# Causal mask of the three-branch attention: added by VectorE head by head with the search for the smallest score, instead of by TensorE products

## The chip, the core and the metric

The kernel runs on one core of a Trainium2 chip. The metric is the time of one execution on the device, in microseconds. The kernel before takes 1296.79 us, the median of three runs (1296.17 to 1296.86).

## The reference, cut to what matters

The whole program is a chain of two blocks on 256 tokens of width 1024: four feed-forward layers, an mLSTM mixer, a three-branch attention ("nsa"), and two further attention mixers ("fox" and "dsa"). The change touches only the selected-block branch and the window branch of the three-branch attention. With 256 tokens the 4 blocks of 64 keys are all within the 16 that may be chosen, and the window of 512 covers everything, so both branches are causal attention over all keys, each with its own keys and values:

```python
m_s = (pos <= t[None, :, None, None, None]) & (val >= 0)[..., None]
s_s = jnp.einsum('bqhgd,bqhksd->bqhgks', qq, k_g).reshape(B, Q_BLOCK, N_KVH, G, top * SEL_BLOCK)
p_s = masked_softmax(s_s, m_s.reshape(B, Q_BLOCK, N_KVH, 1, top * SEL_BLOCK))
o_s = jnp.einsum('bqhgn,bqhnd->bqhgd', p_s.astype(dt), ...)
...
m_w = (kpos[None, :] <= t[:, None]) & (kpos[None, :] > t[:, None] - WINDOW) & (kpos[None, :] >= 0)
s_w = jnp.einsum('bqhgd,bkhd->bqhgk', qq, k_w)
p_w = masked_softmax(s_w, m_w[None, :, None, None, :])
o_w = jnp.einsum('bqhgk,bkhd->bqhgd', p_w.astype(dt), v_w)
return (gb[:, :, 0, :, :, None] * o_c + gb[:, :, 1, :, :, None] * o_s
        + gb[:, :, 2, :, :, None] * o_w)
```

There are 16 query heads in 4 groups that share keys, with 64 columns a head. `masked_softmax` subtracts the row's largest score, takes the exponential, sets masked places to 0 and divides by the row's sum. The kernel holds the scores with their sign turned, so it looks for the smallest and adds 1e30 where a key is masked.

## The kernel before, in words

The program is written by hand, engine by engine: each of TensorE, VectorE, ScalarE (ACT), GpSimd and SyncE has one list of instructions in fixed order, and semaphores tie the lists together. Nothing is scheduled by a planner. Most of the time goes to weight products: each weight piece is loaded, split by ScalarE into a high part (`whi`, line 1573) and by VectorE into a low part (`wlo`, line 2112), and multiplied by TensorE in three passes (lines 694, 695, 697).

The three-branch attention works in 12 units (`n_units`, line 493), here called unit 0 to unit 11. Units 0 to 3 belong to the first 128 tokens, one per key group; each holds 8 heads (4 of each branch) of 128 by 128 scores. Units 4 to 11 belong to the second 128 tokens, one per key group and branch; each holds 4 heads of 128 by 256 scores. A unit's scores fill two of PSUM's eight banks, half of the heads in each; even units have banks 0 and 1, odd units 2 and 3.

For each unit the engines do this:

- TensorE, `n_scores` (line 1305): two mask products (line 1320), which write the mask into the unit's two banks by multiplying a 128 by 128 identity with the mask, and then the heads' score products (line 1325), which add onto it. Identity and mask lie in the tile GH; ScalarE copies them there once (lines 1876 and 1877). From unit 2 on the products wait for the exponentials of the unit two before, which had the same banks.
- VectorE, `n_least_of` (line 2692): one reduction over the whole unit (line 2695), which gives the smallest score of each row and head.
- ScalarE, `n_exps` (line 1917): one exponential per head out of PSUM into SBUF (line 1924), with the row sums. All of them wait for the reduction.
- VectorE, `n_scale` (line 2697): reciprocal of the sums (2703), times the gates (2705 or 2708), and one product over the unit (2710).
- TensorE, `n_turn` (line 1329): eight transposes (line 1339) into banks 4 and 5. ScalarE copies the first out (line 1931), VectorE the second (`n_second_of_pt`, line 2715). Then `n_values` (line 1354) multiplies by the values.

VectorE's list in the loop (line 2730) is, for k from 0: scale unit k, least of unit k+2, copy of unit k's second transposed half; TensorE's is scores of unit k+2, transposes of unit k, values of unit k-1. Between these stand pieces of the third, compressed branch (lines 2665 to 2690 on VectorE, 1282 to 1303 on TensorE), and, once, the first half of the result leaves PSUM: after unit 4 TensorE's `cmp_values` (1301) ends the first 128 tokens' sums, ScalarE copies them out (1937), and VectorE takes their low part (2737). At the end stand, on TensorE, the transposes of units 10 and 11, the rest of the compressed branch, two values, and then the output projection.

The fox and dsa stages, later in the program, mask in another way: `mask_four` (line 2260) issues one `tensor_tensor_reduce` per head (line 2268), which adds the mask to a head's scores out of PSUM, writes the sums into SBUF and returns their smallest. In the trace this is a pair of instructions, CUSTOM_DVE_ANT_0 and DVE_READ_ACCUMULATOR2_ANT.

Of the kernel before, what the change touches and what calls it, by code (L numbers as in the profile page):

```python
# [19 lines left out]
ALU = mybir.AluOpType  # L20
ACT = mybir.ActivationFunctionType
AX = mybir.AxisListType.X

P = 128
# [15 lines left out]
BIG = 1e30  # L40
# [66 lines left out]
def program(nc, a, out):  # L107
# [20 lines left out]
    for name in order:  # L128
# [6 lines left out]
        else:  # L135
            w, chunks = stages[name]
# [5 lines left out]
    with ExitStack() as ctx:  # L142
        def sb(name, shape, dt=F32):
            return ctx.enter_context(nc.sbuf_tensor(name, shape, dt))

        def sem(name):
            return ctx.enter_context(nc.semaphore(name))
# [13 lines left out]
        GH = sb("GH", [P, 2, T], F32R)  # L161
# [23 lines left out]
        nmin = sb("nmin", [P, 96])  # L185
# [11 lines left out]
        ident = con[:, C_ID:C_ID + P]  # L197
        caus = con[:, C_CAUS:C_CAUS + 256]
# [4 lines left out]
        def carve(start, *sizes):  # L203
            views, at = [], start
            for n in sizes:
                views.append(arena[:, at:at + n])
                at += n
            assert at <= AW, (at, AW)
            return views
# [17 lines left out]
        KTS, VTS, KB, VB, v_k, v_kd, v_cd, v_ct, v_sc, v_scT = carve(  # L227
            0, 2 * KVH * T, 2 * NT * T, KVH * 64, 2 * KVH * P, 1024, 2048, 2048, 2048, 256, 256)
        KTS = KTS.rearrange("p (b h t) -> p b h t", b=2, h=KVH)
# [140 lines left out]
        q_ps = sem("q_ps")  # L370
        n_ps = sem("n_ps")
        n_in = sem("n_in")
        n_const = sem("n_const")
        n_score = sem("n_score")
        n_least = sem("n_least")
        n_exp = sem("n_exp")
# [114 lines left out]

        q_bank = (0, 1, 4, 5)
        n_units = [(0, g, None) for g in range(KVH)] + [(1, g, b) for g in range(KVH) for b in range(2)]
        n_ident, n_later = GH[:, 0, 0:P], GH[:, 0, P:2 * P]

        def n_bank(t, c):

# [2 lines left out]
        def n_rows(k):  # L500

            return (8, P) if k < KVH else (4, T)

        def n_cols(k):

            at = 8 * k if k < KVH else 4 * k + 4 * KVH
            return slice(at, at + n_rows(k)[0])

        def n_slot(k, b, j):

            return 4 * (j % 2) + 2 * b + j // 2 if k < KVH else 2 * (j % 2) + j // 2

        def n_score_banks(k):

            n, w = n_rows(k)
            return PS[:, 2 * (k % 2):2 * (k % 2) + 2, :].rearrange("p b n -> p (b n)").rearrange("p (j s) -> p j s", j=n)

        def n_weights(k):

            n, w = n_rows(k)  # L520
            return wide[:, 1024 * (k % 2):1024 * (k % 2) + 1024].rearrange("p (j s) -> p j s", j=n)
# [160 lines left out]
        def _(pe):  # L682
            mm, tr = nc.tensor.matmul, nc.tensor.transpose
# [392 lines left out]
            o = side("m_rows")  # L1076
# [8 lines left out]
            for name, sums in (("m_a", (grow[2], grow[0])), ("m_floor", (grow[1],))):  # L1085
                o = side(name)
# [218 lines left out]
            def n_scores(k):  # L1305

                t, g, one = n_units[k]
                if k == 0:
                    pe.wait_ge(n_const, 1)
                    pe.wait_ge(n_in, 4)  # L1310
                elif k == 1:
                    pe.wait_ge(n_in, 6)
                else:
                    pe.wait_ge(n_exp, k - 1)
                if k == KVH:
                    pe.wait_ge(qT_act, 2)
                    pe.wait_ge(qT_dve, 2)
                o, (n, w) = n_score_banks(k), n_rows(k)
                for m in range(2):
                    mm(o[:, n // 2 * m:n // 2 * m + n // 2, P * t:P * t + P], n_ident,  # L1320
                       n_later.unsqueeze(1).to_broadcast([P, n // 2, P]), start=True, stop=False, skip_group_check=True)
                for b in range(2) if one is None else (one,):
                    for j in range(4):
                        half = slice(64 * (j % 2), 64 * (j % 2) + 64)
                        last = mm(o[:, n_slot(k, b, j), :], n_qT[half, 2 * g + j // 2, t * P:t * P + P],
                                  KTS[half, b, g, 0:w], start=False, stop=True, skip_group_check=True)
                last.then_inc(n_score, 1)

            def n_turn(k):
# [66 lines left out]
            k = len(n_units) - 2  # L1396
# [16 lines left out]
            o = side("f_rows")  # L1413
# [35 lines left out]
            for t in range(NT):  # L1449
                for c in range(3):  # L1450
                    n, end = stages["dsa"][1][c][2], chunk_end("dsa", c)
                    if t == 0 and c == 0:
# [4 lines left out]
                        o = PS[:, dsa_bank(0, 0), 0:n]  # L1457
# [21 lines left out]
            for w in range(2):  # L1479
                o = side(f"qi{w}")  # L1480
                for i in range(2):
                    for t in range(NT):
                        m = 2 * w + i
# [4 lines left out]
            o = side("kr")  # L1488
# [3 lines left out]
            o = side("ki_ckv")  # L1492
# [32 lines left out]
            for j in range(4):  # L1525
                o = side(f"dk{j}")
                for i in range(2):
                    last = mm(o[:, i * T:i * T + T], d_wukr[:, 2 * j + i, :], d_ckvT, start=True, stop=True,
                              skip_group_check=True)
# [29 lines left out]
        def _(act):  # L1559
            A = nc.scalar.activation  # L1560
# [157 lines left out]
            o = even_bank("mlstm", 0)  # L1718
# [12 lines left out]
            o = side("m_rows")  # L1731
# [10 lines left out]
            o = even_bank("mlstm", 3)  # L1742
            A(m_qT[:, 0:2, :], two(o), ACT.Copy).then_inc(chunk_act, 1)
            o = side("m_floor")
# [16 lines left out]
            o = even_bank("mlstm", 4)  # L1761
# [40 lines left out]
            o = even_bank("kv", 0)  # L1802
# [70 lines left out]


            turn("nsa")
            A(n_ident, ident, ACT.Copy)
            A(n_later, caus[:, P:2 * P], ACT.Copy).then_inc(n_const, 1)
            root_of("nsa")
            first = first_piece["nsa"]

# [36 lines left out]
            def n_exps(k):  # L1917

                if k >= 2:
                    act.wait_ge(n_turned, k - 1)  # L1920
                act.wait_ge(n_least, k + 1)
                o, c = n_score_banks(k), n_cols(k).start
                for j in range(n_rows(k)[0]):
                    last = A(n_weights(k)[:, j, :], o[:, j, :], ACT.Exp, scale=-1.0, bias=nmin[:, c + j:c + j + 1],
                             accum_out=zsum[:, c + j:c + j + 1])
                last.then_inc(n_exp, 1)
# [51 lines left out]
            o = even_bank("fox", 0)  # L1978
            A(f_f[:, 0, :], o[:, 336:344], ACT.Copy)
            A(f_v[:, 0, 688:1024], o[:, 0:336], ACT.Copy).then_inc(chunk_act, 1)  # L1980
            o = even_bank("fox", 1)
# [9 lines left out]
            o = side("f_rows")  # L1991
            A(grow[1], o[0:HEADS, 0:T], ACT.Identity, bias=bif[:, 2:3]).then_inc(side_act, 1)
            log_forget(1)
            o = even_bank("fox", 2)
            A(f_v[:, 0, 344:688], o[:, 0:344], ACT.Copy).then_inc(chunk_act, 1)
            silu_sigmoid("fox", 3, 0)
            for c in (4, 5):
                o = even_bank("fox", c)
                A(f_qT[:, 4 * (c - 4):4 * (c - 4) + 2, :], two(o), ACT.Copy, scale=-float(P) ** -0.5)\
                    .then_inc(chunk_act, 1)  # L2000
            for c in (6, 7):
                o = even_bank("fox", c)
# [40 lines left out]
            o = side("qi0")  # L2043
            A(d_qiT[:, 0:2, :], two(o), ACT.Copy).then_inc(side_act, 1)
            o = even_bank("dsa", 3)
            A(xs[:, 0, 512:1024], o, ACT.Copy).then_inc(chunk_act, 1)
            o = side("ki_ckv")
# [21 lines left out]
            for j in (0, 2):  # L2069
                o = side(f"dk{j}")  # L2070
# [4 lines left out]
            for j in range(4):  # L2075
                if j == 2:
                    exps_four("dsa", 0)
                o = side(f"dv{j}")
# [19 lines left out]
        def _(dve):  # L2098
            V = nc.vector
# [257 lines left out]
            o = odd_bank("mlstm", 0)  # L2357
# [60 lines left out]
            o = side("m_a")  # L2418
# [3 lines left out]
            o = odd_bank("mlstm", 3)  # L2422
# [12 lines left out]
            o = odd_bank("mlstm", 4)  # L2435
# [83 lines left out]
            o = odd_bank("kv", 0)  # L2519
# [171 lines left out]

            def n_least_of(k):

                dve.wait_ge(n_score, k + 1)
                V.tensor_reduce(nmin[:, n_cols(k)], n_score_banks(k), AX, ALU.min).then_inc(n_least, 1)

            def n_scale(k):

# [67 lines left out]
            o = odd_bank("fox", 0)  # L2766
            V.tensor_copy(f_f[:, 1, :], o[:, 336:344])
            V.tensor_copy(f_v[:, 1, 688:1024], o[:, 0:336]).then_inc(chunk_dve, 1)
            o = odd_bank("fox", 1)
# [26 lines left out]
            o = odd_bank("fox", 2)  # L2796
# [13 lines left out]
            for c in (4, 5):  # L2810
                o = odd_bank("fox", c)
# [5 lines left out]
            for c in (6, 7):  # L2817
                o = odd_bank("fox", c)
# [89 lines left out]
            o = side("qi1")  # L2908
# [16 lines left out]
            o = side("kr")  # L2925
# [54 lines left out]
            for j in (1, 3):  # L2980
                o = side(f"dk{j}")
# [61 lines left out]
```

## Time and profile before

| what | us |
|---|---|
| median of the runs | 1296.79 |
| the profiled execution | 1295.36 |
| its span, first to last instruction | 1293.6 |
| TensorE busy in the span | 1267.7 |
| VectorE busy | 872.2 |
| ScalarE busy | 615.9 |

The profiled execution is one execution with the hardware profiler on; its time is the device's, and its span is what the trace covers. The units of the change stand from about 766 to 824 us of the span. TensorE counts as busy while a product is in its pipeline, so a busy TensorE is not one at its peak; its clock has two levels, 1.2 and 2.4 GHz, which the profile shows as a granted share of 0.5 and 1. On VectorE an instruction's duration overlaps the next one's start by some 0.07 us, so the time that an instruction takes from its engine is read from start to start.

### The profile page before, as it was taken

How to read it: one execution, taken by the hardware profiler on the slowest of the kernel's cores; microseconds unless marked ns; L12 is line 12 of the kernel's file. 1: busy time of each engine (PE TensorE's matmuls, PEld its weight loads, DVE VectorE, ACT ScalarE, POOL GpSimd, SP SyncE). 2: the span in 40 equal slices, each digit the busy share in tenths (PEclk: the TensorE clock that was granted, in tenths of full speed). 3: DMA queues.
4: the chain of work that ended last, by engine and by line, in shares of the span. 5: the costliest groups of instructions: out<-in, count | busy, mean ns of one | idle time of the engine just before them, and what ended most of it. 6: DMA issues, size and time to landing. Idle time of an engine off the chain costs nothing.

```text
span 1293.6 us, 16507 instructions
## 1 busy us (share of the span) xinstructions
PE 1267.7 (98%) x6723; PEld 1075.0 (83%) x6723; DVE 872.2 (67%) x1314; ACT 615.9 (48%) x842; POOL 19.2 (1%) x35
## 2 busy tenths in 40 slices
PE   8999999999999999999999998999999999999997
PEld 6888888988888888888888876788888899988876
DVE  7655557887655557685757669765555567576896
ACT  6434436535434446454544456664344353544471
POOL 2000000100000000000000000000000000000000
PEclk9999999999999999999999989999999999999999
DMA  9665545444655555566574340065555686446401
GB/s 330 222 195 194 182 149 185 162 140 153 214 186 195 187 184 164 181 196 199 174 245 165 135 163 1 15 226 180 179 185 192 133 225 173 146 140 221 162 1 66
DMA packets 158812, 218.17 MB, mean 169 GB/s; under 512 B 8257, under 2 KB 110993, under 8 KB 158737
## 3 DMA queue, kind: packets, MB, share of 16 engines
q1 hardware_dynamic: 157168, 213.33, 51.3%
q0 software_dynamic: 1376, 3.71, 1.0%
q8 instruction: 53, 0.87, 0.3%
q14 instruction: 23, 0.18, 0.0%
q10 hardware_dynamic: 192, 0.08, 0.0%
HBM read 216.04 MB, written 1.05 MB: 168 GB/s over the span
## 4 chain that ended last, share of the span: by engine, by line
PE 88%; DVE 7%; ACT 1%; issue 1%; DMA 1%; SPq 1%; DVEq 0%
PE PS L694 25%; PE PS L697 24%; PE PS L695 24%; PE PS L729 2%; PE PS L736 2%; PE PS L730 2%; PE PS L844 2%; PE PS L714 1%; DVE wlo L2112 1%; PE PS L1055 1%; PE PS L1339 1%; DMA raw<-in_ffn_w_out_dram 1%; DVE arena L2710 1%; SPq L602 1%; DVE d_work L2959 1%
## 5 line engine op out<-in xcount | busy, mean ns | idle before, releaser
L2112 DVE TENSOR_TENSOR wlo<-raw,whi 128x2048 fp32r<-128x2048 f32 (+4 forms) x205 | 455.1, 2230 | 125.5 <-ACT whi L1573 124.9
L1573 ACT ACTIVATE whi<-raw 128x2048 fp32r<-128x2048 f32 (+4 forms) x205 | 379.6, 1864 | 69.2 <-DMA raw<-in_fox_w_in_dram 32.3
L694 PE MATMUL PS<-whi,XL 128*128 128x512 f32 (+4 forms) x976 | 378.2, 388 | 2.2 <-DVE wlo L2112 1.3
L695 PE MATMUL PS<-wlo,XH 128*128 128x512 f32 (+4 forms) x976 | 372.6, 383 | 0.0
L697 PE MATMUL PS<-whi,XH 128*128 128x512 f32 (+4 forms) x976 | 259.5, 383 | 0.0
L694 PEld LDWEIGHTS PS<-whi,XL 128*128 128x128 f32 x976 | 183.4, 188 | 36.4 <-DVE wlo L2112 2.1
L695 PEld LDWEIGHTS PS<-wlo,XH 128*128 128x128 f32 x976 | 183.6, 188 | 32.4
L697 PEld LDWEIGHTS PS<-whi,XH 128*128 128x128 f32 x976 | 181.7, 189 | 34.6
L1629 ACT ACTIVATE scr<-PS,rn 128x256 f32<-128x256 f32 x88 | 41.7, 474 | 224.4 <-PE PS L697 223.9
L694 PE MATMUL PS<-whi,GL 128*128 128x512 f32 x320 | 125.4, 392 | 0.0
L695 PE MATMUL PS<-wlo,GH 128*128 128x512 f32 x320 | 124.6, 389 | 0.0
L2212 DVE SCALAR_TENSOR_TENSOR scr<-PS,rn,scr 128x256 f32<-128x256 f32 x88 | 42.4, 482 | 92.6 <-ACT scr L1629 92.4
L697 PE MATMUL PS<-whi,GH 128*128 128x512 f32 x320 | 98.7, 390 | 0.0
L1634 ACT ACTIVATE GH<-PS 128x512 fp32r<-128x512 f32 x40 | 23.9, 599 | 156.4 <-PE PS L844 156.4
L694 PE MATMUL PS<-XH,wlo 128*128 128x256 f32 x320 | 81.5, 287 | 1.2 <-ACT xs L2079 1.2
L695 PE MATMUL PS<-XL,whi 128*128 128x256 f32 x320 | 80.2, 283 | 0.0
L2221 DVE TENSOR_TENSOR GL<-PS,GH 128x512 fp32r<-128x512 f32 x40 | 27.7, 691 | 73.7 <-ACT GH L1634 73.6
L697 PEld LDWEIGHTS PS<-whi,GH 128*128 128x128 f32 x320 | 60.1, 188 | 12.6
L695 PEld LDWEIGHTS PS<-wlo,GH 128*128 128x128 f32 x320 | 60.1, 188 | 12.1
L694 PEld LDWEIGHTS PS<-whi,GL 128*128 128x128 f32 x320 | 60.1, 188 | 12.2
L694 PEld LDWEIGHTS PS<-XH,wlo 128*128 128x128 f32 x320 | 61.3, 192 | 2.9 <-ACT xs L2079 2.0
L695 PEld LDWEIGHTS PS<-XL,whi 128*128 128x128 f32 x320 | 61.3, 192 | 0.1
(402 smaller groups left out, 1360.3 us busy)
## 6 DMA issues: line engine op xcount, KB each, us to landing
raw<-in_ffn_w_in_dram SPq DMA_DIRECT2D x174, 512.0 KB, 4.9
raw<-in_ffn_w_out_dram SPq DMA_DIRECT2D x88, 512.0 KB, 4.9
raw<-in_fox_w_in_dram SPq DMA_DIRECT2D x24, 512.0 KB, 8.1
raw<-in_a_w_in_dram SPq DMA_DIRECT2D x16, 512.0 KB, 4.5
raw<-in_dsa_w_in_dram SPq DMA_DIRECT2D x16, 512.0 KB, 4.9
raw<-in_kv_w_dram SPq DMA_DIRECT2D x12, 512.0 KB, 4.2
raw<-in_fox_w_in_dram SPq DMA_DIRECT2D x12, 344.0 KB, 5.1
raw<-in_a_w_out_dram SPq DMA_DIRECT2D x8, 512.0 KB, 4.6
```

Of the source, the lines that this page charges most:

```text
L694: mm(o, xl, wh, start=start and i == 0, stop=False, skip_group_check=True)
L695: mm(o, xh, wl, start=False, stop=False, skip_group_check=True)
L697: last = mm(o, xh, wh, start=False, stop=stop and i == len(terms) - 1, skip_group_check=True)
L729: mm(o, xh, wl, start=opens and i == 0 and j == 0, stop=False, skip_group_check=True)
L730: mm(o, xh, wh, start=False, stop=False, skip_group_check=True)
L736: last = mm(o, XL[:, k, t * P:t * P + P], wh, start=False, stop=stop and j == len(ks) - 1, skip_group_check=True)
L844: last = tr(PS[:, 6, k * T + t * P:k * T + t * P + P], ffg[:, t, k * P:k * P + P], ident)
L1573: A(whi[:, p % SLOTS, 0:n], raw[:, p % SLOTS, 0:n], ACT.Copy).then_inc(hi_done, 1)
L1629: A(ffe[:, t, :], PS[:, gate_bank(f, i, t), 0:FC], ACT.Sigmoid, scale=rn[:, t:t + 1]).then_inc(exp_done, 1)
L2112: V.tensor_tensor(wlo[:, p % SLOTS, 0:n], raw[:, p % SLOTS, 0:n], whi[:, p % SLOTS, 0:n].bitcast(F32), ALU.subtract).then_inc(lo_done, 1)
L2212: V.scalar_tensor_tensor(out=g, in0=both[:, 0:FC], scalar=rn[:, t:t + 1], in1=e, op0=ALU.mult, op1=ALU.mult).then_inc(silu_step, 1)
L2221: V.tensor_tensor(to[:, :, :], two(PS[:, 6, :]), hi_[:, :, :].bitcast(F32), ALU.subtract)\
```

## The change

TensorE no longer writes the mask: the two mask products per unit go, and each score product now opens its own sum (`start=True`). ScalarE no longer copies identity and mask into GH, and the semaphore for that goes. VectorE's one reduction per unit becomes one `tensor_tensor_reduce` per head, 64 in all: it reads the head's scores from PSUM, adds the mask from the constants in SBUF, writes the masked scores back to the same place in PSUM and returns their smallest. For the first 128 tokens the mask is one triangle of 128 columns; for the second, 128 columns of zero and the triangle, so all 256 columns pass through. Each of these counts up the semaphore `n_least`, and ScalarE now waits for it twice per unit, once for each half of the heads, which is one bank.

```diff
@@ n_scores, TensorE
                 if k == 0:
-                    pe.wait_ge(n_const, 1)
                     pe.wait_ge(n_in, 4)
...
                 o, (n, w) = n_score_banks(k), n_rows(k)
-                for m in range(2):
-                    mm(o[:, n // 2 * m:n // 2 * m + n // 2, P * t:P * t + P], n_ident,
-                       n_later.unsqueeze(1).to_broadcast([P, n // 2, P]), start=True, stop=False, skip_group_check=True)
                 for b in range(2) if one is None else (one,):
                     for j in range(4):
                         half = slice(64 * (j % 2), 64 * (j % 2) + 64)
                         last = mm(o[:, n_slot(k, b, j), :], n_qT[half, 2 * g + j // 2, t * P:t * P + P],
-                                  KTS[half, b, g, 0:w], start=False, stop=True, skip_group_check=True)
+                                  KTS[half, b, g, 0:w], start=True, stop=True, skip_group_check=True)
                 last.then_inc(n_score, 1)
@@ ScalarE, before the stage
             turn("nsa")
-            A(n_ident, ident, ACT.Copy)
-            A(n_later, caus[:, P:2 * P], ACT.Copy).then_inc(n_const, 1)
             root_of("nsa")
@@ n_exps, ScalarE
                 if k >= 2:
                     act.wait_ge(n_turned, k - 1)
-                act.wait_ge(n_least, k + 1)
                 o, c = n_score_banks(k), n_cols(k).start
                 for j in range(n_rows(k)[0]):
+                    if j % (n_rows(k)[0] // 2) == 0:
+                        act.wait_ge(n_least, c + j + n_rows(k)[0] // 2)
                     last = A(n_weights(k)[:, j, :], o[:, j, :], ACT.Exp, scale=-1.0, bias=nmin[:, c + j:c + j + 1],
@@ n_least_of, VectorE
+                t, c, o = n_units[k][0], n_cols(k).start, n_score_banks(k)
                 dve.wait_ge(n_score, k + 1)
-                V.tensor_reduce(nmin[:, n_cols(k)], n_score_banks(k), AX, ALU.min).then_inc(n_least, 1)
+                for j in range(n_rows(k)[0]):
+                    V.tensor_tensor_reduce(o[:, j, :], o[:, j, :], caus[:, P - P * t:2 * P], 1.0, BIG * 4, ALU.add, ALU.min,
+                                           nmin[:, c + j:c + j + 1]).then_inc(n_least, 1)
```

## Rows read from the trace of the kernel before

**Rows 1.** busy us of each engine and granted clock in two stretches

```profile
766.00:774.00 8.00, 7.24 (x47) 5.35 (x48) 6.16 (x8) 5.03 (x20) 0.00 (x0) 0.68 0.61 192
774.00:826.00 52.00, 47.96 (x372) 34.20 (x372) 45.21 (x72) 36.58 (x133) 0.00 (x0) 1.00 0.01 1
```

**Rows 2.** chain of waits from 766 us: start, duration, engine, tile, line

```profile
766.42 1.03 PE PS L1320 x2
767.45 2.03 PE PS L1325 x16
...
769.58 1.24 DVE nmin L2695
...
770.84 2.91 ACT arena L1924 x16
```

**Rows 3.** groups of TensorE by line, 766 to 826 us: the mask products

```profile
L1320 PE MATMUL PS<-GH 128*128 128x256 f32 (+1 forms) x24 | 7.8, 411 | 0.8 <-ACT arena L1924 0.8
```

**Rows 4.** VectorE in time, 769-782 us: start, duration, operation, idle before

```profile
769.58 1.23 DVE L2695 TENSOR_REDUCE nmin<-PS 128x8 f32<-128x1024 f32 x1 [1.15 <-PE PS L1325]
...
772.05 1.22 DVE L2695 TENSOR_REDUCE nmin<-PS 128x8 f32<-128x1024 f32 x1 [0.65 <-PE PS L1325]
...
773.85 0.19 DVE L2703 RECIPROCAL rz<-zsum 128x8 f32<-128x8 f32 x1
...
775.66 1.22 DVE L2695 TENSOR_REDUCE nmin<-PS 128x8 f32<-128x1024 f32 x1 [0.16 <-PE PS L1325]
776.81 0.68 DVE L2715 COPY arena<-PS 128x512 f32<-128x512 f32 x1
...
780.25 1.22 DVE L2695 TENSOR_REDUCE nmin<-PS 128x8 f32<-128x1024 f32 x1
781.52 0.69 DVE L2715 COPY arena<-PS 128x512 f32<-128x512 f32 x1
```

**Rows 5.** VectorE in order of time, 789 to 800 us

```profile
789.08 1.23 DVE L2695 TENSOR_REDUCE nmin<-PS 128x4 f32<-128x1024 f32 x1
790.34 0.69 DVE L2715 COPY arena<-PS 128x512 f32<-128x512 f32 x1
...
797.98 0.69 DVE L2737 TENSOR_TENSOR XL<-PS,XH 128x512 fp32r<-128x512 f32 x1 [1.40 <-ACT XH L1937]
798.66 1.22 DVE L2695 TENSOR_REDUCE nmin<-PS 128x4 f32<-128x1024 f32 x1
799.80 0.68 DVE L2715 COPY arena<-PS 128x512 f32<-128x512 f32 x1
```

**Rows 6.** VectorE in order of time, 815 to 818 us

```profile
815.04 1.22 DVE L2695 TENSOR_REDUCE nmin<-PS 128x4 f32<-128x1024 f32 x1 [0.29 <-PE PS L1325]
816.18 0.68 DVE L2715 COPY arena<-PS 128x512 f32<-128x512 f32 x1
...
817.18 1.23 DVE L2710 TENSOR_TENSOR arena<-arena,rz 128x1024 f32<-128x1024 f32 x1
```

**Rows 7.** TensorE in order of time: one waiting transpose, the last mask, the tail

```profile
789.21 1.09 PE L1339 MATMUL PS<-con,arena 128*128 128x128 f32 x8 [0.17 <-DVE arena L2710]
...
813.43 0.50 PE L1320 MATMUL PS<-GH 128*128 128x256 f32 x2
...
818.52 1.04 PE L1339 MATMUL PS<-con,arena 128*128 128x128 f32 x8
```

**Rows 8.** VectorE's mask and minimum in the fox stage, 128 columns a head

```profile
1120.64 0.28 DVE L2268 CUSTOM_DVE_ANT_0 arena<-PS,arena 128x128 f32<-128x128 f32 x1
...
1122.32 0.08 DVE L2268 DVE_READ_ACCUMULATOR2_ANT nmin<- 128x1 f32 x1
```

**Rows 9.** the same in the dsa stage, 256 columns a head

```profile
1249.51 0.42 DVE L2268 CUSTOM_DVE_ANT_0 arena<-PS,arena 128x256 f32<-128x256 f32 x1
...
1252.27 0.09 DVE L2268 DVE_READ_ACCUMULATOR2_ANT nmin<- 128x1 f32 x1
```

More of the change, by code:

```diff
@@ L372, in program @@
         n_in = sem("n_in")
-        n_const = sem("n_const")
         n_score = sem("n_score")
@@ L493, in program @@
         n_units = [(0, g, None) for g in range(KVH)] + [(1, g, b) for g in range(KVH) for b in range(2)]
-        n_ident, n_later = GH[:, 0, 0:P], GH[:, 0, P:2 * P]
         def n_bank(t, c):
```

## The prediction

> **What bounds the kernel now.** I read the page of the profile first, then the granted clock and busy time by stretch, then the chain of waits through the twelve units, and last VectorE and TensorE in order of time. The page shows TensorE busy through nearly the whole span, so the question is only which engine paces the 58 us in which the twelve units run. In the main stretch VectorE is busy 45.2 of 52 us at full TensorE clock; TensorE reads 48.0, but its transposes have to wait [rows 1]. A transposed unit waits for VectorE's product over it: eight transposes begin after 0.17 us of idle that VectorE ended, and VectorE takes the copy right after them [rows 5, 7]. VectorE has waits of its own at only a few places: for scores at the first three units and the last (1.15, 0.65, 0.16, 0.29 us), and 1.40 us for the copy of the first tokens' result [rows 4 to 6]. So the loop is paced by VectorE's list, with the turn from VectorE to TensorE and back inside it. The mask products are 24 records with 7.8 us of busy time [rows 3], mostly where TensorE would wait anyway; they stand on the path only before unit 0, where the chain shows 1.03 us of mask, then 2.03 us of scores, then the reduction, then the exponentials [rows 2], and in front of the other scores that VectorE waits for.
>
> **What a unit's minimum costs afterwards.** The trace has this instruction with its output in SBUF: eight heads of 128 columns from 1120.64 to 1122.32, so 0.21 us a head [rows 8]; eight heads of 256 columns from 1249.51 to 1252.27, so 0.345 us [rows 9]. A unit of eight heads then takes 1.68 us and one of four 1.38 us. The reduction takes 1.14 or 1.15 us from its start to the next instruction's where the copy is ready (775.66 to 776.81, 798.66 to 799.80), and 1.26 or 1.27 us where the copy waits for the transposes (789.08 to 790.34, 780.25 to 781.52) [rows 4, 5]. An output in PSUM is nowhere in the trace; I take the SBUF rows as they are the same instruction, and bound it below.
>
> **The sum, along VectorE's list** (minus is earlier).
> - Start: the 1.03 us of mask before unit 0's first score go. VectorE, free since 768.43 (769.58 less 1.15), starts at 768.55: -1.03.
> - Unit 0: 1.68 for 1.15, +0.53. It then was free at 771.40 and waited until 772.05 for unit 1's scores; now it is free at 770.90, and these scores are ready by 768.45 + 2.03 = 770.5 even at the low clock. So unit 1 starts 1.15 earlier.
> - Unit 1: +0.53, so unit 0's scaling starts at 773.85 - 0.62 = 773.23. The exponentials that it needs: the first four heads are done at 768.55 + 0.84 + 0.08, and 2.91 us of exponentials [rows 2] end at 772.4. In time. The half-unit wait lets them start 1.4 us earlier, but from here nothing on VectorE waits for them.
> - Unit 2: its 0.16 us wait goes (-0.78), its minimum costs +0.53: -0.25.
> - Unit 3: 1.68 for 1.27, +0.41: now +0.16. The early start is used up.
> - Units 4 and 5: 1.38 for 1.26, +0.12 each: +0.40. Unit 6's +0.12 falls into the 1.40 us idle at 797.98, which is counted from unit 4's scaling, before it: still +0.40.
> - Units 7 and 8: 1.38 for 1.14, +0.24 each: +0.88. In this place the transposes were long done.
> - Units 9 and 10: +0.12 each: +1.12.
> - Unit 11: VectorE waited 0.29 for its scores, which come 0.5 us of mask earlier [rows 6, 7], so -0.29, then +0.24: +1.07.
> - Unit 10's scaling ends at 817.18 + 1.23 + 1.07 = 819.48; its transposes stood at 818.52 and now start at about 819.5: +1.0. What follows on TensorE is the tail of the stage and the weight products, which all move by that.
>
> ScalarE's two copies into GH go; it waited for VectorE behind them, so that is worth nothing. Its second wait per unit holds up the other half's exponentials and behind them its copy of the transposed half; the second half of the heads takes 0.84 or 0.69 us, less than the four or two exponentials in front of it, so it costs nothing. The TensorE time freed in units 2 to 10 (5 us of the 7.8) only lengthens its waits.
>
> The sum is +1.0 us, against an execution of 1295.36, so 1296.4; against the median of the runs, 1296.79, it is 1297.8. The three runs lie within 0.7 us.
>
> **Bounds of the unseen price.** A head's cost enters the sum 60 times: 32 heads in units 0 to 3, 28 in units 4, 5 and 7 to 11. From above: if the pair doesn't overlap its neighbours, a head takes its whole durations, 0.28 + 0.08 and 0.42 + 0.09 us [rows 8, 9], 0.15 and 0.165 more: 32 x 0.15 + 28 x 0.165 = 9.4 us, so 1307.2. From below: the same elements can hardly pass faster than in the one reduction, 1.15 us a unit. Then the early start stays: -1.15 at unit 1, -0.16 and -0.29 for the two waits, so -1.6 us and 1295.2; a loss is possible, a gain over that not, since TensorE's transposes and the copies pace the loop then. I stay at the SBUF rows.
>
> **Rivals.**
> - Slower: the write to PSUM puts a fixed price on each head. The place is VectorE's list in all units but 6; it decides from 27 ns a head (1.6 us over 60), since +2.6 us is 0.2%, about what a measurement of this kernel can tell from no change. For it: the change makes 64 short instructions of 12 long ones, and no row shows a write into PSUM by VectorE. Against it: reading from PSUM costs nothing extra in rows 8 and 9, and the durations there hold 0.07 us of overlap. With 50 ns, a third of the upper bound, it is 60 x 0.05 = 3.0 more: 1300.8.
> - The early start is kept (heads cheaper than in the fox rows): 1295.2 as above. For it: ScalarE's exponentials start 1.4 us earlier. Against it: rows 8 and 9 are the same instruction.
> - TensorE's clock falls: it already did between 766 and 774 us (0.68 of full speed), after a run of short products at the end of the projection [rows 1]. Without the masks TensorE has some 43 of 53 us busy (48 less 5); at half speed it needs 1.6 us for one, and paces the loop. A stretch like that one, 5 us at the low level, costs 0.6 x 5 = 3 us more: 1300.8. Against it: the clock stayed full through stretches in which TensorE waited.
>
> The Trainium skill speaks against this change too: "VectorE: DVE Perf Modes", in its section on the TRN2 errata, has each VectorE instruction pay a fixed latency that large tiles spread out, with 120 cycles plus one per element for a PSUM source. From that page one would estimate 258 and 392 ns a head, some 48 ns more than the rows, and the sum would be +3.8 us. The rows 8 and 9, also with a PSUM source, are below it at 210 and 345 ns, so here the trace does not agree, and it is evidence for the slower rival only as far as the PSUM write is new.
>
> **Chances.** The forecast (between -0.6 and +2.6 us, by heads from just under the SBUF rows to 27 ns over them) has 0.62; the PSUM price 0.24; the early start kept 0.10; the clock 0.04. Faster by over 0.2% would need 2.6 us, more than the cheapest head can give, so I leave it 0.05; the rest of the early-start case falls within 0.2%. Within 0.2%: 0.68. Slower: 0.27. The range runs from 1295.4, the early start kept, to 1301.8, a head some 65 ns dearer, and leaves out the dearest heads.
>
> **What would show it.** Right: on the new minimum's line, pairs 0.21 and 0.345 us apart from start to start; unit 0's first one near 768.5; unit 3's copy of a transposed half, which stood at 781.52 behind its minimum, within 0.3 us of that; idle of TensorE's transposes grown; unit 10's transposes near 819.5. The PSUM rival: pairs further apart. The clock rival: a granted clock below 1 after 774 us. The early-start rival: unit 10's transposes before 818.5. The forecast is wrong if these transposes lie more than 2.6 us from where they were, or if a part of the program before 766 or after 826 us changes its length.

## The result, and the profile after

The kernel after takes 1301.1 us, the median of five runs (1300.74 to 1304.11); the kernel before took 1296.79 beside it. The ratio is 1.0041 with a 95% interval of 1.0026 to 1.0056: slower by 5.3 us (3.4 to 7.3; the two medians differ by 4.3). The profiled execution takes 1300.97 us with a span of 1298.8, against 1295.36 and 1293.6.

In the two profiled executions nearly all of it arises in the stretch of the change. I measure that stretch between two instructions of VectorE that the change leaves alone: the sum of squares in front of the query norm, and the low part of the output projection's input for the second 128 tokens. First before, then after:

```profile
762.46 1.22 DVE L2647 TENSOR_REDUCE ss<-scr 128x16 f32<-128x1024 f32 x1 [1.60 <-ACT scr L1895]
829.18 1.22 DVE L2291 TENSOR_TENSOR XL<-PS,XH 128x1024 fp32r<-128x1024 f32 x1
```

```profile
762.24 1.22 DVE L2640 TENSOR_REDUCE ss<-scr 128x16 f32<-128x1024 f32 x1 [1.61 <-ACT scr L1887]
834.15 1.22 DVE L2284 TENSOR_TENSOR XL<-PS,XH 128x1024 fp32r<-128x1024 f32 x1
```

The stretch is 66.72 us before and 71.91 after, +5.19; the span grew by 5.2. The execution's time grew by 5.6, so 0.4 us lie outside the span, and no run tells why. VectorE after, in order of time (start, duration, line, output and input, idle before), shows both halves of the cause:

```profile
768.24 0.30 DVE L2690 CUSTOM_DVE_ANT_0 PS<-PS,con 128x128 f32<-128x128 f32 x1
...
768.46 0.33 DVE L2690 CUSTOM_DVE_ANT_0 PS<-PS,con 128x128 f32<-128x128 f32 x1
768.71 0.14 DVE L2690 DVE_READ_ACCUMULATOR2_ANT nmin<- 128x1 f32 x1
768.71 0.33 DVE L2690 CUSTOM_DVE_ANT_0 PS<-PS,con 128x128 f32<-128x128 f32 x1
...
782.52 0.30 DVE L2690 CUSTOM_DVE_ANT_0 PS<-PS,con 128x128 f32<-128x128 f32 x1 [1.79 <-PE PS L1319]
...
787.84 0.42 DVE L2690 CUSTOM_DVE_ANT_0 PS<-PS,con 128x256 f32<-128x256 f32 x1
...
788.19 0.47 DVE L2690 CUSTOM_DVE_ANT_0 PS<-PS,con 128x256 f32<-128x256 f32 x1
788.57 0.14 DVE L2690 DVE_READ_ACCUMULATOR2_ANT nmin<- 128x1 f32 x1
788.57 0.47 DVE L2690 CUSTOM_DVE_ANT_0 PS<-PS,con 128x256 f32<-128x256 f32 x1
...
816.03 0.43 DVE L2690 CUSTOM_DVE_ANT_0 PS<-PS,con 128x256 f32<-128x256 f32 x1 [0.42 <-PE PS L1319]
```

Heads of 128 columns follow each other by 0.25 us and heads of 256 by 0.38, where the same instruction with its output in SBUF has 0.21 and 0.345 [rows 8, 9]. Only the first head of each unit, at 768.24 or 787.84, takes hardly longer than those: 0.22 and 0.35 us. And VectorE waits 1.79 us for the scores of unit 3, for which it did not wait before [rows 4]. TensorE after, in order of time, shows why these are late:

```profile
764.23 1.05 PE L695 MATMUL PS<-whi,XH 128*128 128x48 f32 x8
765.21 2.06 PE L1319 MATMUL PS<-arena 64*128 64x128 f32 x32
767.20 1.09 PE L1277 MATMUL PS<-con,xs 128*128 128x128 f32 x8
772.34 2.08 PE L1319 MATMUL PS<-arena 64*128 64x128 f32 x16 [4.05 <-ACT arena L1917]
775.21 1.94 PE L1333 MATMUL PS<-con,arena 128*128 128x128 f32 x8 [0.80 <-DVE arena L2706]
776.94 3.52 PE L1283 MATMUL PS<-arena 128*128 128x64 f32 x16
780.39 2.08 PE L1319 MATMUL PS<-arena 64*128 64x128 f32 x16
...
811.23 1.52 PE L1333 MATMUL PS<-con,arena 128*128 128x128 f32 x8 [1.74 <-DVE arena L2706]
...
823.50 1.04 PE L1333 MATMUL PS<-con,arena 128*128 128x128 f32 x8
```

The scores of units 0 and 1 are done at 767.2: the masks are gone, and in this execution the clock is full from 764 to 768 us, where before it was at 0.50 from 766 to 770. TensorE then has eight transposes, waits 4.05 us for the exponentials of unit 0, and comes back slow: unit 2's 16 score products take 2.08 us, as long as 32 of them had taken at 765.21. The windows of the kernel after (busy time of PE, PEld, DVE, ACT, POOL, then the granted clock) say that the clock was at its low level:

```profile
766.00:774.00 8.00, 3.95 (x48) 3.59 (x44) 7.86 (x40) 5.85 (x24) 0.00 (x0) 0.80 0.58 188
774.00:826.00 52.00, 44.02 (x306) 31.87 (x305) 47.06 (x154) 31.62 (x125) 0.00 (x0) 0.87 0.00 1
...
770.00:786.00 16.00, 12.87 (x78) 11.36 (x80) 13.85 (x67) 11.16 (x57) 0.00 (x0) 0.57 0.03 10
786.00:810.00 24.00, 18.85 (x146) 12.53 (x142) 22.27 (x71) 15.64 (x59) 0.00 (x0) 1.00 0.00 1
810.00:816.00 6.00, 4.77 (x25) 2.86 (x26) 5.48 (x14) 2.78 (x11) 0.00 (x0) 0.72 0.02 5
```

Before, 774 to 826 us ran at 1.00 [rows 1]; now it has 0.87, with low pieces in 770 to 786 and 810 to 816 us. The second piece also follows a wait of TensorE: 1.74 us at 811.23. Before, the same transposes had waited 1.10 us, the longest wait of TensorE in that stretch:

```profile
807.38 1.09 PE L1339 MATMUL PS<-con,arena 128*128 128x128 f32 x8 [1.10 <-DVE arena L2710]
```

### The profile page after: what moved, and what is told of

Same layout as the page of the kernel before. It is cut to its first block, busy times and chain, and to the rows that moved or that the text cites. A ratio compares the mean times of both kernels' runs of the same rounds, so it can differ in the third digit from the quotient of the medians.

```text
span 1298.8 us, 16572 instructions
## 1 busy us (share of the span) xinstructions
PE 1265.6 (97%) x6699; PEld 1074.6 (83%) x6699; DVE 878.1 (68%) x1430; ACT 615.8 (47%) x840; POOL 19.1 (1%) x35
## 3 DMA queue, kind: packets, MB, share of 16 engines
HBM read 216.04 MB, written 1.05 MB: 167 GB/s over the span
## 4 chain that ended last, share of the span: by engine, by line
PE 88%; DVE 7%; ACT 1%; issue 1%; DMA 1%; SPq 1%; DVEq 0%
PE PS L692 25%; PE PS L693 24%; PE PS L695 24%; PE PS L727 2%; PE PS L734 2%; PE PS L728 2%; PE PS L842 1%; PE PS L712 1%; DVE PS L2690 1%; PE PS L1053 1%; DMA raw<-in_ffn_w_out_dram 1%; DVE arena L2706 1%; SPq L600 1%; PE PS L1333 1%; DVE wlo L2105 1%
```

## The experiments

Twelve kernels, each run 5 to 12 times beside the kernel before, which took 1296.67 us (median) beside the first four, 1295.91 beside the next four and 1296.54 beside the last; the ratios are to these. "Stretch" is the one defined above, from one profiled execution of each, against 66.72 us before; a median is over all its runs, so the two need not agree.

| kernel | median us | ratio (95%) | stretch us | against before |
|---|---|---|---|---|
| after | 1301.1 | 1.0041 (1.0026 to 1.0056) | 71.91 | +5.19 |
| masks kept | 1301.89 | 1.0043 (1.003 to 1.0056) | 70.34 | +3.62 |
| TensorE's part alone | 1296.76 | 1.0005 (0.9994 to 1.0016) | 65.90 | -0.82 |
| heads to SBUF | 1300.12 | 1.0028 (1.0018 to 1.0038) | 70.87 | +4.15 |
| gap filled | 1300.73 | 1.0033 (1.0022 to 1.0045) | 69.80 | +3.08 |
| SBUF and gap filled | 1298.16 | 1.0022 (1.0013 to 1.0031) | 67.43 | +0.71 |
| SBUF and masks kept | 1299.83 | 1.0033 (1.002 to 1.0045) | 70.00 | +3.28 |
| one wait | 1301.8 | 1.0041 (1.0029 to 1.0054) | 71.34 | +4.62 |
| ScalarE's second copy | 1296.33 | 0.9999 (0.999 to 1.0008) | 64.77 | -1.95 |
| wide gate products | 1295.61 | 1.0 (0.999 to 1.0011) | 67.02 | +0.30 |
| wide, second copy | 1294.79 | 0.9988 (0.9979 to 0.9996) | 64.68 | -2.04 |
| SBUF, filled, second copy | 1298.33 | 1.0019 (1.001 to 1.0028) | 68.87 | +2.15 |
| the same, and wide | 1294.95 | 0.999 (0.9982 to 0.9999) | 65.79 | -0.93 |

**Masks kept.** The mask products stay on TensorE as dead work, and with them ScalarE's two copies.

```diff
                 o, (n, w) = n_score_banks(k), n_rows(k)
+                for m in range(2):
+                    mm(<the mask's place>, n_ident, <n_later, repeated>, start=True, stop=True, ...)
```

> The changed kernel, with the two mask products per unit put back on TensorE as dead work: the score products then overwrite what they wrote, and VectorE still adds the mask. Theory P (each head's instruction on VectorE costs more when it writes into PSUM: 0.25 us for 0.21 at 128 columns, 0.38 for 0.345 at 256, times 60 heads on the path = 2.2 us) expects the changed kernel's loss to stay, and the 1.03 us of mask before unit 0 to be back on the path: 1300 to 1301.5. Theory C (without the mask products TensorE's clock falls: 770.6 to 785 and 811.8 to 815.2 us at half speed in the changed kernel, 764 to 771 us before) expects the clock as before, low once near 764 to 771 us and full in the loop, and 1297.5 to 1299. Both at work: near 1300, with a full clock after 772 us and heads still 0.25 and 0.38 us apart.

VectorE's waits before the first scores came back (0.62 and 0.35 us), and the clock was low where it was before, and only there:

```profile
764.00:770.00 6.00, 6.00 (x34) 4.47 (x35) 5.07 (x21) 1.92 (x4) 0.00 (x0) 0.56 1.02 334
770.00:786.00 16.00, 12.61 (x110) 9.85 (x110) 15.34 (x74) 13.46 (x68) 0.00 (x0) 0.95 0.03 12
```

Its stretch is 1.6 us shorter than after's, though TensorE does more; its median is no better (the profiled execution, 1299.19 us, is the shortest of its five). So 3.62 us of loss need no lower clock in the loop: there is a cost on VectorE besides.

**TensorE's part alone.** The kernel before without mask products and ScalarE's two copies; no mask at all is applied in it.

```diff
-                for m in range(2):
-                    mm(<the mask's place>, n_ident, ..., start=True, stop=False, ...)
...
-                                  KTS[half, b, g, 0:w], start=False, stop=True, ...)
+                                  KTS[half, b, g, 0:w], start=True, stop=True, ...)
```

> The kernel before, without the mask products and without a mask at all (both branches then attend to later tokens too); VectorE keeps its one reduction per unit. Theory P alone: TensorE's work only shrinks, the three waits for scores go, -1.3 to -1.8 us, so about 1295.2. Theory C: TensorE's clock falls in the loop as in the changed kernel, and the time is 1297.5 to 1299.5 although there is less work and VectorE's list is the same.

Taking the 7.8 us of masks [rows 3] from TensorE gives 0.82 us in the stretch and nothing that the runs can tell; the time lies between the two theories. The gap arises here too, with a low clock behind it, but only a short piece (0.5 from 774 to 776 us, 1.00 again from 778 us): VectorE waits 0.48 us for unit 2's scores and 0.29 us for the transposes behind them.

```profile
774.22 2.08 PE L1319 MATMUL PS<-arena 64*128 64x128 f32 x16 [2.54 <-ACT arena L1916]
```

**Heads to SBUF.** The masked scores go to an SBUF tile (the query tile xs, free from then on), and the exponentials read them there.

```diff
+                if k == 1:
+                    dve.wait_ge(q_ps, 4)
-                    V.tensor_tensor_reduce(o[:, j, :], o[:, j, :], caus[...], ...
+                    V.tensor_tensor_reduce(n_masked(k)[:, j, :], o[:, j, :], caus[...], ...
```

> The changed kernel, with the masked scores of each head written into SBUF (the free query tile xs, two halves in turn) instead of back into PSUM, and the exponentials read there. Theory P: heads 0.21 and 0.345 us apart again as in the fox and dsa stages, 2.2 us less than the changed kernel: about 1298.9. Theory C: the clock falls as in the changed kernel, because TensorE waits for the same exponentials, and the time stays near 1301. Both: between, with pairs at 0.21 and 0.345 us and the same low clock.

```profile
771.59 0.29 DVE L2696 CUSTOM_DVE_ANT_0 xs<-PS,con 128x128 f32<-128x128 f32 x1 [0.93 <-PE PS L1281]
...
776.15 0.29 DVE L2696 CUSTOM_DVE_ANT_0 xs<-PS,con 128x128 f32<-128x128 f32 x1
776.36 0.28 DVE L2696 CUSTOM_DVE_ANT_0 xs<-PS,con 128x128 f32<-128x128 f32 x1
...
783.06 0.29 DVE L2696 CUSTOM_DVE_ANT_0 xs<-PS,con 128x128 f32<-128x128 f32 x1 [1.79 <-PE PS L1323]
...
788.61 0.42 DVE L2696 CUSTOM_DVE_ANT_0 xs<-PS,con 128x256 f32<-128x256 f32 x1
788.96 0.42 DVE L2696 CUSTOM_DVE_ANT_0 xs<-PS,con 128x256 f32<-128x256 f32 x1
```

```profile
775.75 1.94 PE L1337 MATMUL PS<-con,arena 128*128 128x128 f32 x8 [2.10 <-DVE arena L2712]
```

The heads are back at 0.21 and 0.345 us, so the output in PSUM is what made them dearer, by 37 to 40 ns for each head that follows another. (The edit changes two things at once: the memory, and that the scores no longer go back to the place that they were read from. No run separates these.) A wait of 1.79 us for unit 3's scores is still there. TensorE's gap before unit 2's scores was only 1.04 us in this execution; the low clock begins behind a wait of 2.10 us, at 775.75. And the edit adds a wait of its own: unit 1's heads wait 0.93 us until TensorE has read the query tile.

**Gap filled.** After with 16 unused 512-column products in TensorE's gap before unit 2's scores.

```diff
                 q_turned(1, half, 6 + half)
+            for _ in range(16):
+                mm(PS[:, 5, :], XH[:, 0, 0:P], <XH, 512 columns>, start=True, stop=True, ...)
             for k in range(len(n_units) - 2):
```

> The changed kernel, with 16 dead products of 512 columns on TensorE into a free bank, put into the 4.05 us in which TensorE waits for unit 0's exponentials (768.3 to 772.3 us). Theory C: the clock no longer falls there, the 1.79 us for which VectorE waited at unit 3's scores goes, and the time is 1.5 to 2.5 us under the changed kernel's: about 1299. Theory P: nothing but TensorE's waiting time is filled, so 1301.

```profile
771.79 3.90 PE L1373 MATMUL PS<-XH 128*128 128x512 f32 x16
775.62 1.16 PE L1319 MATMUL PS<-arena 64*128 64x128 f32 x16
```

```profile
770.00:786.00 16.00, 13.85 (x117) 11.23 (x114) 15.72 (x80) 12.36 (x62) 0.00 (x0) 0.98 0.15 49
786.00:810.00 24.00, 18.35 (x140) 12.44 (x140) 22.27 (x71) 14.99 (x56) 0.00 (x0) 1.00 0.00 1
810.00:816.00 6.00, 4.73 (x25) 2.88 (x25) 5.53 (x14) 2.81 (x11) 0.00 (x0) 0.72 0.02 5
```

Unit 2's scores take 1.16 us again, and VectorE's wait for unit 3 is gone. The stretch falls by 2.11 us (5.19 to 3.08). The low piece at 810 to 816 us, behind a later wait of 1.74 us, is still there, and VectorE still waits for a slow TensorE behind it (0.29 us at 813.06, 0.18 at 816.07). The median hardly moves, and is nearer to theory P's 1301 than to theory C's 1299. In the profiled execution the stretch begins 2.16 us later than after's, at 764.40, which takes the gain back there; of the others no trace was kept.

**SBUF and gap filled.** Both edits together.

```diff
+                mm(PS[:, 5, :], XH[:, 0, 0:P], ...)                      # 16 times
+                    V.tensor_tensor_reduce(n_masked(k)[:, j, :], ...
```

> The kernel after with both suspected costs taken away: the heads write to SBUF (as in the run that does this alone, 0.21 and 0.345 us a head) and 16 unused 512-column products stand in TensorE's gap before unit 2's scores. Theory (PSUM write about 2 us, low clock in the loop about 2 us, own terms of the change about 1 us): both go together, 1297 to 1298.5, that is +0.5 to +1.8 against before; granted clock 1.0 from 772 to 810 us. Rival (a third cause: the new order of waits itself costs 3 us or more whatever the clock and the output): 1299.5 or more.

```profile
770.00:786.00 16.00, 13.21 (x110) 10.60 (x108) 15.56 (x82) 14.32 (x67) 0.00 (x0) 1.00 0.12 40
786.00:810.00 24.00, 19.09 (x146) 13.12 (x147) 22.23 (x73) 15.14 (x51) 0.00 (x0) 1.00 0.01 1
810.00:816.00 6.00, 5.05 (x40) 3.19 (x40) 5.86 (x21) 3.98 (x14) 0.00 (x0) 1.00 0.01 3
```

The clock is full from 772 us to the end of the loop, and the stretch is 0.71 us longer than before: close to the forecast's own sum of +1.0. After's +5.19 can now be added up along VectorE's list:

- 0.71 us that stay when both costs are gone.
- 1.81 us for the output in PSUM. From its first head to the next instruction a unit of eight heads takes 1.95 or 1.96 us against 1.69 here, one of four 1.49 against 1.38; that is 37 ns for 49 of the 60 heads on the path, all but the first of each unit.
- 2.11 us for the first low piece, which filling the gap takes away. VectorE had waited 1.79 us for unit 3's scores in it, and 0.26 for unit 0's transposes.
- 0.7 us for the second low piece, which after and gap filled both have: one copy of transposes and unit 10's heads come that much later, from start to start, than where nothing holds them.

Together 5.3, against 5.19 measured. Without the first low piece it is 3.2 for gap filled (measured 3.08). For heads to SBUF 0.71, 1.0 of the edit's own wait and 2.6 of waits behind its low piece make 4.3 (measured 4.15), from start to start again. So the two costs add, within some 0.15 us. This rests on one execution of each kernel.

The runs show less. The median lies in the range that was expected, but against the kernel before beside it it is 0.22% or 2.9 us longer, above the expected +0.5 to +1.8. In the profiled execution the span is 2.5 us longer: 0.71 in the stretch, 1.31 before it begins and 0.5 behind it, in code that is the same but for ScalarE's two copies ahead of it. So with both causes taken away about half of the runs' loss is left. The mean granted clock of these eleven runs is a little below that of before's beside them (0.9943 against 0.9954 on average), so a part may be low pieces elsewhere; no trace of them was kept.

**SBUF and masks kept.** The edits of these two kernels together.

```diff
+                    mm(<the mask's place>, n_ident, ..., start=True, stop=True, ...)
+                    V.tensor_tensor_reduce(n_masked(k)[:, j, :], ...
```

> The kernel after with the mask products kept as dead work on TensorE and the heads written to SBUF. Theory: the run with the masks kept and PSUM heads starts the output projection 3.4 us later than before; some 2 us of that are the PSUM write, so about +1.5 here: 1297.5 to 1299, and a granted clock of 1.0 from 772 us on, since TensorE has the masks to do in its gap. Rival (the write to PSUM costs nothing at the end of the stage, since TensorE waits anyway): as the run with the masks kept, 1300 to 1302.

```profile
773.45 0.29 DVE L2704 CUSTOM_DVE_ANT_0 xs<-PS,con 128x128 f32<-128x128 f32 x1 [1.38 <-PE PS L1283]
```

Inconclusive. The stretch is +3.28, but 1.38 us of it is a wait of the edit's own: the SBUF tile is the query tile, and TensorE, held up by the masks at the low clock, read it late. Less that wait it would be +1.9 (an estimate), nearer to the theory's +1.5 than to the +3.62 with PSUM heads, and about what these +3.62 less the 1.81 for the output in PSUM give.

**One wait.** ScalarE waits once per unit, as before the change.

```diff
-                    if j % (n_rows(k)[0] // 2) == 0:
-                        act.wait_ge(n_least, c + j + n_rows(k)[0] // 2)
+                act.wait_ge(n_least, c + n_rows(k)[0])
```

> The kernel after with ScalarE waiting once per unit for all heads, as before the change, in place of once per half. The prediction's step: the half waits are worth nothing to VectorE, so 1300.5 to 1302, as the kernel after. Rival: in units 0 to 2 TensorE's scores wait for ScalarE's exponentials, which start about 1 us later with one wait; the gap before unit 2's scores grows from 4 to 5 us and the end comes 0.5 to 1.5 us later: 1302 to 1303.5.

1.0041, the same as after. The half waits make no difference that the runs can tell, as the prediction had it. In the trace unit 2's scores do start 1.0 us later, counted from the start of the stretch (11.09 us behind it, 10.10 in after), as the rival said, but the stretch is not longer. The gap itself is 3.46 us here, since a low clock from 768 to 772 us makes TensorE late into it.

**ScalarE's second copy.** The kernel before, with the second transposed half of units 4 to 11 copied by ScalarE.

```diff
                 A(t_PT[:, k % 2, 0, ...], PS[:, 4, :], ACT.Copy).then_inc(n_pt_act, 1)
+                if k >= 4:
+                    A(t_PT[:, k % 2, 1, ...], PS[:, 5, :], ACT.Copy).then_inc(n_pt_dve, 1)
...
-                n_second_of_pt(k)
+                if k < 4:
+                    n_second_of_pt(k)
```

> The kernel before (masks by TensorE) with the copy of the second transposed half of units 4 to 11 on ScalarE in place of VectorE, 0.60 us of VectorE's list in each. If VectorE's list paces those units: the list falls from 4.0 to 4.2 us a unit to 3.4 to 3.6, and TensorE with 3.8 us a unit paces next, so 0.2 to 0.4 us less a unit over 7 units, 1.5 to 2.5 us less: 1294.2 to 1295.3. Rival: values wait for ScalarE's second copy behind its first (0.7 us later than now), the turn gets longer and the gain is lost: 1296.5 to 1299.

```profile
811.80 1.22 DVE L2697 TENSOR_REDUCE nmin<-PS 128x4 f32<-128x1024 f32 x1 [0.43 <-PE PS L1325]
815.34 1.22 DVE L2697 TENSOR_REDUCE nmin<-PS 128x4 f32<-128x1024 f32 x1 [0.77 <-PE PS L1325]
819.29 0.18 DVE L2705 RECIPROCAL rz<-zsum 128x4 f32<-128x4 f32 x1 [1.19 <-ACT arena L1924]
```

The stretch is 1.95 us shorter: VectorE's list did pace these units, and once it is lighter TensorE and ScalarE come late by turns. The runs show no gain (0.9999); in this execution the stretch began at 765.47, 3.0 us later than before's, and that took it back. Why the other runs show no gain is not shown.

**Wide gate products.** The 48-column products ahead of the stretch, widened to 128 columns of which 80 are thrown away.

```diff
-                        wh, wl = parts_n(p, kn, n)
-                        last = product(o, ...
+                        wh, wl = [[x[:, p % SLOTS, k * n:k * n + 128] for k in range(kn)] for x in (whi, wlo)]
+                        last = product(PS[:, n_bank(t, c), 0:128], ...     # for the 48 columns alone
```

> The kernel before with the 48-column products of the gate projection (two runs of 24, at about 746 and 763 us) widened to 128 columns; the further columns go to unused PSUM. In the traces so far the granted clock falls to the low level behind such a run, behind the second one in most executions, behind the first in some. Theory (the short products bring the clock down): no low clock from 746 to 772 us; scores of unit 0 at full clock, about 2 us less: 1293.5 to 1295. Rival (the clock falls whatever the width, or the wider products cost as much as they save): 1295.7 to 1297.5.

The clock no longer fell behind the second run of these products (1.00 from 764 to 772 us, where before had 0.50 from 766 to 770). But unit 2 then met a gap of 2.71 us and a low clock behind it, as after does:

```profile
764.44 1.06 PE L697 MATMUL PS<-whi,XH 128*128 128x128 f32 x8
...
772.63 1.22 PE L1322 MATMUL PS<-GH 128*128 128x512 f32 x2 [2.71 <-ACT arena L1926]
```

```profile
772.00:776.00 4.00, 3.37 (x19) 2.50 (x20) 1.72 (x5) 4.00 (x21) 0.00 (x0) 0.57 0.00 1
```

Ratio 1.0; in this execution one low piece was traded for another.

**Three candidates.** All are combinations of the edits above. The first is before with the wide products and the second copy; the second is SBUF heads, filled gap and second copy; the third is that with the wide products.

```diff
+ wide gate products; ScalarE's second copy                                   # on the kernel before
+ heads to SBUF; gap filled; ScalarE's second copy                            # on the kernel after
+ heads to SBUF; gap filled; ScalarE's second copy; wide gate products        # on the kernel after
```

> Candidate: the kernel before with the 128-column gate products and ScalarE's second copy for units 4 to 11. The second copy alone shortened the stretch of the twelve units by 2 us in its trace and gave 0.9999 over its runs. If the two add up: 1292.5 to 1294.5. If the clock's savings are lost again: 1295 to 1296.5.

> Candidate from the kernel after: heads written to SBUF, 16 unused products in TensorE's gap, and ScalarE's second copy for units 4 to 11. If VectorE's list paces the units (theory), taking 0.60 us from it in each unit helps more here than in the kernel before, since TensorE has no masks and needs 3.3 us a unit: 2 to 3 us less than without the copy, so 1294.5 to 1296.5. If the turn through ScalarE paces instead: 1297 to 1299.

> Candidate: the run before it (SBUF heads, 16 unused products, ScalarE's second copy) with the 128-column gate products as well. If the short products bring the clock down, another 1 to 2.5 us less: 1292.5 to 1295; if not, as the run without them.

The first and the third are a little faster than before, 0.9988 and 0.999, with intervals that stay below 1. The first lies between its two expected ranges, the third at the upper end of its lower one. The second came out as its rival had it (1297 to 1299), though not shown to be for the rival's reason: its clock was low at 766 to 773 us and again at 790 to 795. The third's windows have no low clock, with TensorE's gap filled and 128-column products ahead of it:

```profile
744.00:772.00 28.00, 27.25 (x182) 23.43 (x180) 19.98 (x68) 14.57 (x31) 0.00 (x0) 1.00 0.55 189
772.00:826.00 54.00, 45.46 (x358) 32.69 (x359) 44.87 (x156) 44.00 (x144) 0.00 (x0) 1.00 0.01 1
```

So the mask on VectorE can be had at no loss, in the runs made here with four helpers (with two or three of them it was 0.2% slower), and the kernel before with two of them is as fast.

## Why the prediction was wrong

The forecast was +1.0 us, within 0.2%; measured are +5.3 us by the ratio (+4.3 by the medians), inside the range and outside "the same". That it lies inside the range is luck: the upper end stood for heads 65 ns dearer, and they came 30 ns dearer on average over the 60; a second rival, given 0.04, brought the rest. In the trace both rivals came true together. The runs separate them only in part: 1.0028 with heads to SBUF, 1.0033 with the gap filled, 1.0022 with both, and the intervals overlap.

- **"An output in PSUM is nowhere in the trace; I take the SBUF rows."** This step failed. A head that writes to PSUM behind another such head takes 37 ns (128 columns) or 38 ns (256 columns) more. Of the 60 heads on the path 49 pay it, 1.8 us, or 30 ns on average, just beyond the 27 ns from which the slower rival was to decide. The bound from above, 9.4 us, held. The Trainium skill's page "VectorE: DVE Perf Modes", in the section on the TRN2 errata, gives 120 cycles plus one per element for a source in PSUM and an output in SBUF, from which the prediction had estimated 258 and 392 ns. That is the case of rows 8 and 9, which are shorter (210 and 345 ns). For an output in PSUM the page's table has no column, so that the change's heads come near its figures (250 and 382 ns) does not confirm it. The rows that I went by differ from the change in the one point that mattered, where the output lies.
- **"TensorE's clock falls", given 0.04.** It fell, for about 17 us (0.57 over 770 to 786 us is 13.8 us at half speed, 0.72 over 810 to 816 is 3.4). What spoke against it, that the clock stayed full through stretches in which TensorE waited, was read from the loop of before, where no wait of TensorE is longer than 1.10 us; the change made one of 4.05. Its price was mis-sized too: 17 us at the 0.6 us lost per us that I had put down would be 10 us, and it cost 2.8: 2.11 for the first 13.8 us, which filling the gap gave back, and 0.7 for the rest. TensorE had slack to be slow in.
- **"The TensorE time freed only lengthens its waits."** True, and that was the trap: the longer wait is followed by the low clock. The sum costed the freed time at nothing.
- **The early start** came as worked out: unit 0's heads at 768.24 (768.55 forecast), unit 1's at 770.80 (770.90), unit 0's scaling at 773.42 (773.23). But it was VectorE's own list that set it: at the full clock the scores of units 0 and 1 were done at 767.2, where the forecast had counted on the low one and on 768.45 for unit 0's. Before unit 2 after was 0.68 us ahead (774.98 against 775.66); at unit 3 it was 2.27 behind (782.52 against 780.25).
- **Unit 3's copy** was to stand within 0.3 us of 781.52 and stood at 784.47; **unit 10's transposes** near 819.5 and stood at 823.50. By the prediction's own test (more than 2.6 us from where they were, 818.52) that refutes it.
- **The half waits, worth nothing:** so in the runs (one wait: 1.0041 as well). ScalarE's two dropped copies were not tried alone.
- **The own terms** of the sum, +1.0: borne out in one execution, by the stretch of the kernel with both costs taken away, +0.71.

What stays open is the part outside the stretch, and with it about half of the loss in the runs. The profiled executions begin the stretch between 762.2 and 765.5 us, though the code ahead is the same but for ScalarE's two copies and the wide products; those that begin after 763.7 have a low clock at about 748 to 756 us. Whether a kernel gets that low piece more often than another, one profile of each can't tell.

## What to carry to other kernels

Take a price from rows whose operands lie where the new ones will lie: an instruction split into many pays the difference nearly as often as it is issued. Before taking work from TensorE, look at how long it will then wait, and what it must do right after: its clock can fall there. And price a slow stretch by the waits that it makes on the engine that paces, not by its length: 17 us at the low clock cost 2.8 us here.

## What the hardware showed that I had not expected

- The price of the output in PSUM is the same for 128 columns as for 256 (250 against 210 ns, 382 against 345), and the first head of a unit does not pay it (0.21 or 0.22 us, and 0.35): it comes with each head that follows another, not with the elements. Whether it is the write to PSUM as such, or writing back to the place that is being read, no run tells.
- The length of a wait alone does not tell whether the clock falls. Behind waits of TensorE of 4.05 (after), 3.46 (one wait) and 2.54 us (TensorE's part alone) it was low. Behind one of 2.71 us it was low in one execution (wide gate products) and full in another (with the second copy as well). It was low behind 2.10 us (heads to SBUF, at 775.75) and full behind 2.15 (gap filled, at 788 us); low behind 1.74 (after) and full behind 1.73 (one wait, at 814.66). With unused products in the gap before unit 2's scores it was full there, in all four kernels that have them, and these scores ran right behind them in 1.16 us for 2.08 (in the last of the four 0.46 us behind).
- At the full clock eight gate products of 128 columns take 1.06 us and eight of 48 columns 1.05.
- The third candidate's eleven runs lie between 1294.42 and 1296.33 us; those of the kernel before, beside them, between 1294.51 and 1303.34. Among these 35 the time goes with the mean granted clock: 0.998 with 1294.51, 0.994 with 1296.7 to 1297.51, 0.989 with 1303.34.
